# Head norms with squares split in two parts, memory heads on four banks, and the last output tile in halves

## The reference, cut to what matters

```python
# block 1: q and k of 12 heads of 64 columns, 1024 tokens
q = rms_norm(b_q.reshape(bn, s, B_HEADS, B_HEAD_DIM), b_q_norm_w)
k = rms_norm(b_k.reshape(bn, s, B_HEADS, B_HEAD_DIM), b_k_norm_w)
# block 1, memory: 4 heads of 128 columns; mq over 1024 tokens, mk and mv over 256
kv = rms_norm(mem, mem_norm_w) @ m_w_kv
mq = rms_norm(m_q.reshape(bn, s, M_HEADS, M_HEAD_DIM), m_q_norm_w)
mk = rms_norm(mk.reshape(bn, MEM_LEN, M_HEADS, M_HEAD_DIM), m_k_norm_w)
# block 2, end
x = x + gate * (y @ w_out)
return rms_norm_2(x, final_gain)      # over the 1024 columns of each token
```

## Time and profile before

| | |
|---|---|
| median of 3 runs | 1887.42 us (1886.19 to 1888.14) |
| profiled execution | 1887.68 us, span 1886.0 us |
| PE matmul busy | 1786.5 us, 95% of the span |
| PE weight loads | 1434.6 us, 76% |
| DVE | 912.4 us, 48% |
| ACT | 630.8 us, 33% |
| POOL | 201.2 us, 11% |
| mean granted TensorE clock | 0.972 of full speed |

### The profile page before, as it was taken

How to read it: one execution, slowest core, us unless ns; L and a number is a source line. 1 busy time by engine, 2 the same in 40 slices (tenths; PEclk the granted TensorE clock), 3 DMA queues, 4 the chain that set the end, 5 groups by cost and what they waited for, 6 DMA issues and landing times. The chain is left out here.

```text
span 1886.0 us, 22119 instructions
## 1 busy us (share of the span) xinstructions
PE 1786.5 (95%) x8828; PEld 1434.6 (76%) x8828; DVE 912.4 (48%) x1500; ACT 630.8 (33%) x1162; POOL 201.2 (11%) x376
## 2 busy tenths in 40 slices
PE   6999998799999999799999999899999999999698
PEld 5787776688887788578888788688887777777486
DVE  5137777645434654374323322367142445656653
ACT  5222226612133333372212211233213353435531
POOL 3000000078700000000000000381000000000000
PEclk9999998999999999899999999899999999999799
DMA  3221100235423210111111111242623111000042
GB/s 135 61 64 38 45 12 12 59 100 178 124 67 115 67 45 23 59 42 43 51 50 45 48 45 42 78 149 78 138 50 92 36 33 34 23 27 31 23 145 101
DMA packets 146432, 123.06 MB, mean 65 GB/s; under 512 B 8843, under 2 KB 132090, under 8 KB 145658
## 3 DMA queue, kind: packets, MB, share of 16 engines
q1 hardware_dynamic: 146330, 121.65, 21.4%
HBM read 108.37 MB, written 13.26 MB: 64 GB/s over the span
## 5 line engine op out<-in xcount | busy, mean ns | idle before, releaser
L81 PE MATMUL psum<-hT,w_parts 128*128 128x512 f32 x3360 | 811.5, 398 | 15.4 <-DVE w_parts L182 9.3
L81 PEld LDWEIGHTS psum<-hT,w_parts 128*128 128x128 f32 x3360 | 633.6, 190 | 164.3 <-issue 21.8
L182 DVE TENSOR_TENSOR w_parts<-w_raw,w_parts 128x1024 fp32r<-128x1024 f32 x104 | 130.1, 1251 | 477.1 <-ACT w_parts L178 476.9
L81 PE MATMUL psum<-h2T,w_parts 128*128 128x512 f32 x1248 | 300.3, 397 | 1.5 <-PEq L2062 1.5
L81 PEld LDWEIGHTS psum<-h2T,w_parts 128*128 128x128 f32 x1248 | 233.7, 190 | 50.7 <-issue 3.2
L81 PE MATMUL psum<-y_high,wp_parts 128*128 128x512 f32 x384 | 129.8, 398 | 9.8 <-DVE wp_parts L1390 9.5
L178 ACT CAST w_parts<-w_raw 128x1024 fp32r<-128x1024 f32 x104 | 108.2, 1040 | 80.7 <-DMA w_raw<-w_in 57.9
L1342 ACT ACTIVATE gate<-psum,cols 128x512 f32<-128x512 f32 x48 | 33.0, 688 | 297.9 <-PE psum L81 297.9
L81 PE MATMUL psum<-w_parts,y_parts 128*128 128x512 f32 x384 | 89.7, 397 | 8.8 <-DVE y_parts L1645 8.8
L379 DVE RECIPROCAL x<-x 128x512 f32<-128x512 f32 x24 | 80.4, 3351 | 33.5 <-ACT x L369 33.5
L81 PEld LDWEIGHTS psum<-y_high,wp_parts 128*128 128x128 f32 x384 | 72.5, 189 | 28.5 <-DVE wp_parts L1390 9.9
(11 more groups left out here) (341 smaller groups left out, 2194.0 us busy)
## 6 DMA issues: line engine op xcount, KB each, us to landing
w_raw<-w_in SPq DMA_DIRECT2D x94, 512.0 KB, 4.0
middle_a<-ada_w SPq DMA_DIRECT2D x32, 384.0 KB, 3.9
w_raw<-w_out SPq DMA_DIRECT2D x16, 512.0 KB, 4.2
qkT<-x SPq DMA_DIRECT2D x8, 512.0 KB, 8.8
w_raw<-m_w_kv SPq DMA_DIRECT2D x8, 512.0 KB, 3.8
base<-x SPq DMA_DIRECT2D x8, 512.0 KB, 4.2
x_kept<-x_ring SPq DMA_DIRECT2D x8, 512.0 KB, 2.6
base<-x_kept SPq DMA_DIRECT2D x8, 512.0 KB, 3.5
```

The costliest lines, as they stand in the source:

```text
L81: last = pe.matmul(out, lhs(a, k), rhs(b, k), start=(k == 0 and n == 0), stop=(k == depth - 1 and n == 2))
L182: dve.tensor_tensor(self.parts[:, u, LO, :, :], self.raw[:, :, :], self.parts[:, u, HI, :, :].bitcast(F32), ALU.subtract).then_inc(self.lo ...
```

## The change

1. **Squares in two parts.** ACT squares into one buffer `sq` (float32), waits for itself, and copies it rounded to float32r into `sq_high`. GpSimd takes the remainder `sq - sq_high` into `sq_low` (new method `remainder`, run by `Dense.gpsimd` behind the other POOL work). PE sums both parts with two float32r matmuls by a float32r copy of the ones matrix, `same`, which ACT makes once at the start of each run with heads.
2. **Later sum.** These two matmuls stand, in a slot of 512 tokens, ahead of its last two depth tiles (behind matmul 18 of 24); in a slot of 256 tokens behind its last product. DVE's part of a head, now `vector_last`, is done one iteration later: behind the next slot's `split_low` and `vector`.
3. **Memory heads.** mq takes banks 1 and 2, mk0 to mk2 and mv0 bank 0, mk3 and mv1 to mv3 bank 3, so that a bank comes up again after four slots.
4. **Output.** PE waits for the second token tile's low part only ahead of that tile's first product. The last token tile is computed and finished in two halves of 512 columns: gate, residual and gain product per half on DVE, squares per half on ACT (the first half's sum, scaled, goes in as the bias of the last root), the last multiplication of one half on DVE and of the other on ACT, and two stores of 256 KB.

```diff
@@ HeadTile
     def scalar(self, act, run, s):
         q = run.heads.index(s)
-        if q >= 2:
-            act.wait_ge(run.summed, q - 1)
-        act.activation(run.sq[:, q % 2, 0:self.width], run.out(s), ACT.Square).then_inc(run.squared, 1)
+        sq, high = run.sq[:, 0:self.width], run.sq_high[:, 0:self.width]
+        if q >= 1:
+            act.wait_ge(run.reduced, q)
+        act.activation(sq, run.out(s), ACT.Square).then_inc(run.squared, 1)
+        act.wait_ge(run.squared, q + 1)
+        if q >= 1:
+            act.wait_ge(run.summed, q)
+        act.copy(high, sq).then_inc(run.rounded, 1)
+
+    def remainder(self, engine, run, s):
+        q = run.heads.index(s)
+        engine.wait_ge(run.rounded, q + 1)
+        if q >= 1:
+            engine.wait_ge(run.summed, q)
+        engine.tensor_tensor(run.sq_low[:, 0:self.width], run.sq[:, 0:self.width],
+                             run.sq_high[:, 0:self.width].bitcast(F32), ALU.subtract).then_inc(run.reduced, 1)
 
     def after(self, pe, run, s):
         q = run.heads.index(s)
-        pe.wait_ge(run.squared, q + 1)
+        pe.wait_ge(run.same_made, 1)
+        pe.wait_ge(run.reduced, q + 1)
         if q >= 2:
             pe.wait_ge(run.rooted, q - 1)
-        pe.matmul(bank(run.core, run.sum_banks[q % 2], 1)[:, 0:self.width], self.same, run.sq[:, q % 2, 0:self.width],
-                  start=True, stop=True).then_inc(run.summed, 1)
+        out = bank(run.core, run.sum_banks[q % 2], 1)[:, 0:self.width]
+        pe.matmul(out, run.same, run.sq_low[:, 0:self.width], start=True, stop=False)
+        pe.matmul(out, run.same, run.sq_high[:, 0:self.width], start=False, stop=True).then_inc(run.summed, 1)
-    def vector(self, dve, run, s):
+    def vector_last(self, dve, run, s):
@@ Dense.tensor
-            product(pe, self.out(s), self.w.lhs(slot.n % 2), rhs, range(1))
-            if s:
-                self.tiles[self.slots[s - 1].n].after(pe, self, s - 1)
-            product(pe, self.out(s), self.w.lhs(slot.n % 2), rhs, range(1, KT // 2))
+            out, lhs, long = self.out(s), self.w.lhs(slot.n % 2), tile.width == HALF
+            before = self.tiles[self.slots[s - 1].n] if s else Tile(None)
+            product(pe, out, lhs, rhs, range(KT // 2))
             for work in self.beside:
                 work.tensor_mid(pe, s)
-            last = product(pe, self.out(s), self.w.lhs(slot.n % 2), rhs, range(KT // 2, KT))
+            product(pe, out, lhs, rhs, range(KT // 2, KT - 2))
+            if long:
+                before.after(pe, self, s - 1)
+            last = product(pe, out, lhs, rhs, range(KT - 2, KT))
             (tile.extra(pe, self, s) or last).then_inc(self.made, 1)
+            if not long:
+                before.after(pe, self, s - 1)
@@ Dense.scalar, at the start
+        if self.heads:
+            act.copy(self.same, self.same_from).then_inc(self.same_made, 1)
@@ Dense.vector
             self.tiles[slot.n].vector(dve, self, s)
+            if s:
+                self.tiles[self.slots[s - 1].n].vector_last(dve, self, s - 1)
             for work in self.beside:
                 work.vector(dve, s)
+        self.tiles[slot.n].vector_last(dve, self, s)
@@ Dense.gpsimd
         for work in self.beside:
             work.gpsimd(pool)
+        for s in self.heads:
+            self.tiles[self.slots[s].n].remainder(pool, self, s)
@@ Middle
-        mqs = [HeadTile(at(4864, j), lambda h, j=j: half(self.mq[:, j, :], h), self.col("mq")[:, j:j + 1], self.ones,
-                        1 / 128, banks=four) for j in range(4)]
+        mqs = [HeadTile(at(4864, j), lambda h, j=j: half(self.mq[:, j, :], h), self.col("mq")[:, j:j + 1],
+                        1 / 128, **on(1, 2)) for j in range(4)]
...
@@ stage_output, PE
-                pe.wait_ge(y_low, 2)
-                w.products(pe, True, *units[:2]).then_inc(made, 2)
+                w.products(pe, True, *units[:2], each=lambda pe, t: pe.wait_ge(y_low, t + 1)).then_inc(made, 2)
...
+                outs, lhs, _, _ = units[TT - 1]
+                for h in range(2):
+                    w.products(pe, False, (outs[h:h + 1], lhs, [h * HALF], HALF)).then_inc(made, 1)
@@ stage_output, ACT, last tile
+                act.activation(half(sq, 0), half(dst[:, last, :], 0), ACT.Square,
+                               accum_out=part[:, 0:1]).then_inc(summed, 1)
+                act.wait_ge(summed, TT)
+                act.activation(part[:, 1:2], part[:, 0:1], ACT.Identity, bias=eps[:, 0:1],
+                               scale=1 / D).then_inc(remains, 1)
+                act.wait_ge(added, TT + 1)
+                act.activation(half(sq, 1), half(dst[:, last, :], 1), ACT.Square,
+                               accum_out=stat[:, 0, last:TT]).then_inc(summed, 1)
...
+                act.activation(row, row, ACT.Copy, scale=stat[:, 1, last:TT]).then_inc(scaled_act, 1)
@@ stage_output, DVE, last tile
+                for h in range(2):
+                    dve.wait_ge(made, TT + h)
+                    rows = bank(core, 2 * (last % 4) + h, 1)
+                    dve.tensor_tensor(rows, rows, half(gate, h), ALU.mult).then_inc(gated, 1)
...
+                dve.reciprocal(stat[:, 1, last:TT], stat[:, 1, last:TT]).then_inc(inverted, 1)
...
+                dve.tensor_scalar(row, row, stat[:, 1, last:TT], None, ALU.mult).then_inc(scaled, 1)
```

More of the change, by code:

```diff
@@ L307, in vector @@
         pass
+    def vector_last(self, dve, run, s):
+        pass
 class MapTile(Tile):
@@ L1597, in _ @@
                 if final:
-                    for t in range(TT - 3, TT):
+                    for t in range(TT - 3, last):
                         store(t)
-                    for s in stored:
-                        sp.wait_ge(s, 16 * TT // 2)
+                    sp.wait_ge(scaled, TT)
+                    sp.dma_start(half(out_tiles[last], 0), half(rows_out[:, side, :], 0)).then_inc(stored[side], 16)
+                    sp.wait_ge(scaled_act, 1)
+                    sp.dma_start(half(out_tiles[last], 1), half(rows_out[:, side, :], 1)).then_inc(stored[side], 16)
+                    for m, s in enumerate(stored):
+                        sp.wait_ge(s, 16 * TT // 2 + (16 if m == side else 0))
             @block.tensor
@@ L1637, in _ @@
                         split(t)
-                    if final and t >= 4:
+                    if 4 <= t < last + 4:
                         root(t - 4)
+                act.wait_ge(added, TT)
+                act.wait_ge(summed, last)
+                act.activation(half(sq, 0), half(dst[:, last, :], 0), ACT.Square,
[6 more added lines that the diff above has]
+                               accum_out=stat[:, 0, last:TT]).then_inc(summed, 1)
+                act.wait_ge(summed, TT + 1)
+                act.wait_ge(remains, 1)
+                act.activation(stat[:, 1, last:TT], stat[:, 0, last:TT], ACT.Sqrt, bias=part[:, 1:2],
+                               scale=1 / D).then_inc(rooted, 1)
+                act.wait_ge(inverted, TT)
+                act.wait_ge(weighed, 2)
+                row = half(rows_out[:, side, :], 1)
+                act.activation(row, row, ACT.Copy, scale=stat[:, 1, last:TT]).then_inc(scaled_act, 1)
             @block.vector
@@ L1664, in _ @@
                     dve.wait_ge(gain_loaded, 16)
-                for t in range(TT):
+                for t in range(last):
                     dve.wait_ge(made, t + 1)
@@ L2889, in __init__ @@
         self.mvT = mergedT[:, 7, :].rearrange("p (j t) -> p j t", j=4)
-        four = ((0, 1), (2, 3))
+        on = lambda *banks: dict(banks=(banks, banks))
         at = lambda first, j: w_in[:, :, first + j * P:first + (j + 1) * P]
@@ L2945, in prepare @@
                  for t in range(TT)]
-        roots = core.over("roots", [P, 2, 2, HALF], c_at)
+        roots = core.over("roots", [P, 3, HALF], c_at)
+        parts = [core.over("sq_parts", [P, HALF], c_at + at, F32R)[:, :] for at in (6144, 8192)]
+        same = core.sb(self.stack, "same", [P, P], F32R)[:, :]
         attention = Attention(core, self.stack, units, self.ident, [core.over("mem_p", [P, 4, 256], c_at + 4096 * i)[:, :, :] for i in range(2)],
@@ L2950, in prepare @@
                                [self.join, modulation, ssm, mem, turn_mv, attention, self.turn_av],
-                               heads=(roots[:, 0, :, :], roots[:, 1, :, :], (4, 5)), eps=self.eps[:, 0:1],
+                               heads=(self.ones, same, roots[:, 2, :], *parts, roots[:, 0:2, :], (4, 5)), eps=self.eps[:, 0:1],
                                ahead=ahead)
```

52 lines of the change are left out of this document (37 added, 15 removed).

## The result

The changed kernel took 1873.03 us (median of 4 runs, 1871.02 to 1876.33) against 1886.81 us of the kernel before (4 runs, 1884.34 to 1888.14): a ratio of 0.9931, 95% interval 0.9918 to 0.9943. Its profiled execution took 1871.02 us (span 1869.2). Sign and mechanism came as forecast; the gain in the first run's heads and the loss in the memory heads were both mis-sized, the first too small and the second too large.

What follows compares the result with a forecast made beforehand. Matmuls fill 95% of the span, so PE bounds the kernel; first run -9.8, memory heads +4.05 and output -3.1 gave -8.85 us, from 1887.68 to 1878.8 us, range 1873.8 to 1884.2.

Steps and rivals of the forecast that it cites:

- the gain in the first run's heads: First run: cheaper sums in 19 plain slots and 4 with transposes, 19 x 0.53 + 4 x 0.38 = -11.6 us.
- the loss in the memory heads: Memory heads of the middle run: longer wait for weights and lower clock outweigh cheaper sums, +4.05 us (0 to +7).
- A map slot takes 5.58 us for 24 matmuls: First run: pace of PE's products, 0.2325 us each, subtracted from slot periods to get a sum's cost.
- the low terms -10.6, 0 and -3.6: Low end of the range: first run -10.6, middle 0, output -3.6 us, given as 1873.8 us.
- the copy of the ones matrix: Middle run, ahead of its first high part: ACT's copy adds 0.25 us.
- The chain: Memory heads, from a square to the next tile's weights: 0.93 us longer (0.63 to 1.8) through rounded copy and remainder.
- the clock's fall at mq3: Memory heads: idle ahead of mq3 grows from 1.16 to 2.6 us and the clock falls, +2.05 us in all.
- a longer stretch at the low clock +0.4: Memory heads, groups up to mq1 and mq2: more time at low clock, +0.4 us each (0 to 0.8).
- The pair rides in the stream: Head slots: two float32r matmuls cost 0.50 us without waiting; rival that they do not ride: 1893.7 us, chance 0.06.
- DVE keeps up: First run: DVE has 10.5 us of work per two slots in 12.2, so no wait for a bank.
- The end of the first run: Behind the first run's last head: last reciprocal 4.4 us behind the square's start instead of 2.60, +1.8 us.
- The output: Output stage: -0.9 us at the start, -2.2 at the end, stores nothing; -3.1 us (-2.0 to -3.9).

Runs made afterwards that it cites:

- high_only: The changed kernel without the remainder of the squares: one matmul a sum, no POOL work for it; 1864.11 us.
- output_only: The kernel before with part 4 of the change (output) alone; 1882.12 us, 0.9976 of the kernel before.
- after_again: The changed kernel, unedited, measured and traced once more; 1873.27 us.
- late_float32: The changed kernel with whole squares and a float32 sum again, at the late place, without rounded copy and remainder; 1877.42 us.
- remainder_dve: The changed kernel with DVE instead of POOL subtracting the remainder; 1881.25 us in one run.
- two_forms: The changed kernel with two-part squares in the first run only, one late float32 sum per memory head in the middle run; 1870.48 us, ratio 0.9909 to the kernel before.
- early_pair: The changed kernel with the pair of sum matmuls where the old sum stood, behind the first depth tile; 1963.13 us in one run.

## Why the prediction was right and where it was wrong

**Which step failed.** First, "A map slot takes 5.58 us for 24 matmuls" as the base of every sum. That slot in the earlier trace rows stands between transposes, and 0.10 us of it belong to the change from products to transposes and back. Another row of the kernel before, which I did not use, has 72 products in one piece:

```profile
65.17 16.64 PE L81 MATMUL psum<-hT,w_parts 128*128 128x512 f32 x72
```

The next instruction starts at 81.64, so these are 81.64 - 65.17 = 16.47 us, 0.229 a matmul and 5.49 a slot; high_only gives 5.48. With it the old plain sum costs 1.13 us instead of 1.03, and with the pair at 0.46 instead of 0.50 its replacement saves 0.67 instead of 0.53. In the four slots with transposes the base drops out, and there 0.40 was measured for 0.38. So 19 x 0.67 + 4 x 0.40 = 14.3 us against 11.6; the trace has 14.24. Of these 2.6 us 1.9 are the base (19 x 0.10) and 0.8 the pair (19 x 0.04). The base alone would have put the forecast and both ends of its range 1.9 us lower, the low end at 1871.9, and the measured 1873.03 within it. Two slips of arithmetic are beside that: the low terms -10.6, 0 and -3.6 give 1873.5, which is not 1873.8 by rounding, and with 0.465 for the pair the gain is 12.4, not 12.3.

**Second, the memory heads**, +3.8 forecast without the copy of the ones matrix, 0 and +2.1 in the two traces against the one of the kernel before. Cut at the squares (second square of one mq to the first of the next, and from mq3's second to the scores):

| | mq0 to mq1 | to mq2 | to mq3 | to scores | each half, x4 |
|---|---|---|---|---|---|
| before | 16.71 | 16.85 | 15.30 | 15.49 | 6.59 |
| output_only | 16.92 | 15.13 | 15.20 | 15.49 | 6.59 |
| forecast | +1.28 | +1.28 | +2.58 | +0.8 | -0.53 |
| changed | +0.62 | -0.91 | +2.17 | +0.72 | -0.66 |
| after_again | +0.83 | +0.81 | +2.19 | +0.90 | -0.66 |

The rows of forecast, changed and after_again are differences to the kernel before; the other two are lengths. output_only has the same heads as the kernel before, and in its trace the clock stayed up at mq2 (behind 1.91 us of idle; it fell behind 2.01 in the kernel before). Traces in which the clock fell at the same places give the change's own price: the first trace of the changed kernel against output_only +1.6 us (90.67 - 89.09), after_again against the kernel before +2.1. That is about half of the 3.8 that I had forecast.

The chain is as forecast (0.79 to 1.09 for 0.93, place by place; 0.25 for 0.3 where the low part meets the remainder), and so is the clock's fall at mq3, the largest price, in both traces (in high_only it stayed up there behind the same 2.15 us of idle). The step that failed is "a longer stretch at the low clock +0.4": where the clock fell in both, the stretch from mq1's first product to its first square is no longer than before (595.87 - 588.21 = 7.66 us, and 7.85 before). Place by place, after_again lies under the forecast by 0.45 and 0.47 us at the first two groups, 0.39 at mq3 and 0.5 in the four halves, and 0.1 over it ahead of the scores. The halves carry the first error again (0.5 us in four). And in the first trace the clock stayed up at mq2, behind the longest idle of the three (6.07 us to its first square instead of 7.66); that is luck of an execution, worth 1.6 us, and not an effect of the change. The idle times were 2.85, 3.04 and 2.15 us (forecast 3.3, 3.5, 2.6), in part because PE now waits 0.28 to 0.33 us for the late low part already ahead of mk0, which I had not seen.

**Right by its steps.** The pair rides in the stream (0.46 for 0.50, remainder 1.26 to 1.30 us for 1.2, handoffs of 0.03 to 0.11), and no slot of the first run waits for POOL. DVE keeps up: no slot of the first run waits for a bank, and the reciprocals took 3.35 us with the remainder running inside them, as the rule of the Trainium skill (SBUF — State Buffer, Who interferes with whom) has it for one SBUF input; the low part that starts inside the remainder (1.47 instead of 1.22 us) shows the other side of the rule. The end of the first run cost +1.6 (up to +2.1 in other traces) for +1.8. The output gave 1.04, 2.06 and 0.2 to 0.4 us for 0.9, 2.2 and nothing; the smaller stores, which I took as nothing, landed a little sooner (2.2 us from issue for 256 KB, 3.1 for 512 KB in the earlier trace rows). No table load came between the last square and the root.

**The sum.** Heads -14.2, their end +1.6, turn +0.7, memory +1.6 to +2.1, output -3.5: -13.3 to -13.8, against 13.8 and 14.0 us by the medians of two measurements. The forecast missed 2.6 us in the heads and 1.7 to 2.2 in the memory heads, both to the same side.

**What stays open.** The turn to the middle run is 0.7 us longer in both traces of the changed kernel, where 0.25 was forecast; as a whole it scatters (73.5 to 75.3 us over the traces, 73.86 and 74.49 with the old heads). One wait in it is steady. PE's idle time ahead of the first product there is 4.28 us before (4.29 in output_only), 5.02 in the changed kernel, 4.52 in high_only, late_float32 and remainder_dve, which have no head work on POOL, and 4.83 in two_forms, which has it in the first run only and lacks the copy (there I had expected 4.5 or 5.0). So 0.2 us are the copy of the ones matrix, and some 0.5 us come with POOL's instructions in the first run; what waits for them at the turn was not found. Nor was what decides whether the clock falls ahead of an mq.

## What to carry to other kernels

Take the pace of a stream from a stretch with no other instruction in it, or from two variants that differ by one; a slot between transposes had 0.10 us in it that belonged to the transposes, and multiplied by 19 that is more than the terms that I took pains over. Compare a stage only between traces in which the clock fell at the same places. A longer chain is free where the engine behind it has other work until it ends (the remainder in the first run), and paid where that engine already waits for it (the copy ahead of the next weights): ask in each stage which of both it is, and give each stage its own form if they differ, as two_forms does. When a consumer is moved later, look at what its buffers now hold up (the banks, 9.9 us here); when work ahead of a wait is reordered, ask who stands behind it now.

## What the runs showed of the hardware that I had not expected

- In these traces the length of PE's idle time does not alone decide whether its clock falls. The 18 matmuls behind it took 4.42 us behind 3.04 us of idle and 5.96 behind 2.15 in the changed kernel, and 4.42 behind 2.15 at the same place of high_only; in two_forms 5.98, 4.38 and 5.96 us behind 2.50, 2.54 and 1.81.
- A wait of 2.05 us in each plain slot brought the clock down in 15 of 19 of them, and such a slot is 3.9 us longer; the four in which the clock stayed up are 2.3 us longer (early_pair).
- A float32 pair of matmuls between float32r products costs 0.84 us where a float32r pair costs 0.46.
- POOL and DVE hold each other up both ways: DVE's low part took 1.47 instead of 1.22 us behind a started remainder, and POOL's remainder 1.78 instead of 1.29 behind a started low part.
